# Weight sums for the modulation: computed and moved by GpSimd instead of VectorE and SyncE

## The chip, the cores and the metric

One NeuronCore of one Trainium2 chip runs the whole program. The metric is the device time of one execution, in microseconds (us). Before the change the median of 3 runs is 3883.19 us (3877.04 to 3884.56). Engines are named as in the profile: PE (TensorE matmul), PEld (its weight load), DVE (VectorE), ACT (ScalarE), POOL (GpSimd), SP (SyncE, which here only issues DMAs).

## The reference

A token sequence of 256 x 1024 goes through `first_block` (two layers: a gated feed-forward, an RWKV-7 and attention mixer, a second feed-forward) and then through `second_block` (two layers with a modulation of the norms and residuals, and a mixture over 16384 experts). What the change touches is small:

```python
# second_block, per layer l; c and c_ctx have 1024 elements, mod_w[l] is 1024 x 6144
m  = jax.nn.silu(c)     @ mod_w[l] + mod_b[l]     # 6 rows of 1024
mc = jax.nn.silu(c_ctx) @ mod_w[l] + mod_b[l]     # only layer 0, only its first 2048 columns
```

`m` does not depend on `x`, so the kernel makes most of it during `first_block`.

## The kernel before, in words

Activations lie with 128 tokens on the partitions. A large product streams its weights: `stream` (L581) takes one weight tile after another through two raw buffers (`raw_weights`, slots u = 0 and 1). For each tile SP issues the load, ACT rounds it to a high part (L634), DVE subtracts to get the low part (L658, both tiles of SBUF are read), and PE multiplies high and low parts (L449 to L451, three matmuls for each product). SP may load tile t+2 into a slot once DVE has made the low part of tile t. ACT may write the high part of tile t+2 once PE is done with tile t.

A feed-forward (`swiglu`, L816) is two such streams with 11 tiles each. The first (`linear_turned_stage`, ffn_in, 2 MB a tile, two DMAs) also has, for each tile, two sigmoid-gates on ACT and six DVE operations that finish `hidden` and its two parts. The second (`linear_sum_stage`, ffn_out, 1 MB a tile) accumulates in PSUM and adds to the residual at its end. `first_layer` (L1594) calls `swiglu` twice, and is run for l = 0 and 1 by a hardware loop. So there are eight feed-forward streams; here they are called A (first ffn_in), B (first ffn_out), C (second ffn_in) and D (second ffn_out), in each of the two layers.

`SideSums` (L529) works beside these four streams. The modulation weights of layer l are cut into 24 tiles of 128 x (8 x 256), 1 MB each. Partition p of block k holds row 128k + p. For each tile the eight blocks are multiplied by the partition's own condition value (`k.cond`, column k) and summed to 128 x 256; the sum over the partitions follows much later (`modulations`, L1655). The first 8 tiles are also summed with a second set of conditions (for `ctx`). Before the change the tiles are split 6, 6, 6, 6 over A, B, C and D, so A has 6 tiles with two sums, B has 2 with two sums and 4 with one, C and D have 6 with one.

The order is written out by hand. DVE makes a side tile after the low part and the finish of a weight tile: a `tensor_scalar` and seven `scalar_tensor_tensor` for each sum, 128 x 256 each. SP, after the load of weight tile t, waits in `SideSums.step` for side tile t-2 to be summed, loads the side tile two further on, and stores the sums to HBM:

```python
for t in range(2, tiles):
    load(t, t % 2, t // 2)      # waits for DVE's low part, issues the weight tile
    side.step(sp, t - 2)        # waits for DVE's side sum, issues load and stores
```

All its semaphores are in the set that POOL clears at the end of each stage (`k.clear`). A stage is a block at whose end all engines meet. POOL has no work in any of these stages. Later, in `experts` (L2117), it issues the 512 indirect DMAs that gather expert rows.

Of the kernel before, what the change touches and what calls it, by code (L numbers as in the profile page):

```python
# [11 lines left out]
ALU = mybir.AluOpType  # L12
# [3 lines left out]
P = 128  # L16
D = 1024
SEQ = 256
NT = SEQ // P
KC = D // P  # L20
# [12 lines left out]
NF = D_FF // P  # L33
# [90 lines left out]
class Ops:  # L124
# [3 lines left out]
    def __init__(self, nc, eng, vector):  # L128
        self.nc, self.eng, self.on_vector = nc, eng, vector
# [74 lines left out]
class Kernel:  # L204


    def __init__(self, nc, ctx, sems):
        self.nc, self.ctx = nc, ctx
        self.sem, self.names = Semaphores(nc, ctx, sems), 0

        self.rows = [ctx.enter_context(nc.semaphore(f"row{r}")) for r in range(RING)]
        self.row_uses = [0] * RING


        self.arrived = [ctx.enter_context(nc.semaphore(f"arrived{u}")) for u in range(2)]
        self.fills = [0, 0]
        self.preloaded = False
# [311 lines left out]
class SideSums:  # L529

    COLS = 256

    def __init__(self, k, tiles, sums, ctx_sums, which, both, room):
        self.k, self.tiles, self.sums, self.ctx_sums, self.which, self.both = k, tiles, sums, ctx_sums, which, both
        self.w, self.acc = room

    def load(self, sp, i):  # L540
        if i < len(self.which):
            sp.dma_start(self.w[:, i % 2, :], self.tiles[self.which[i]]).then_inc(self.k.sem[f"side_in{i % 2}"], 16)

    def stores(self, i):
        return 16 * sum(1 + (n < self.both) for n in self.which[:i])

    def step(self, sp, i):
        if i >= len(self.which):
            return
        sp.wait_ge(self.k.sem["side_done"], i + 1)  # L550
        self.load(sp, i + 2)
        n = self.which[i]
        cs = slice(n * self.COLS, (n + 1) * self.COLS)
        sp.dma_start(self.sums[:, cs], self.acc[:, i % 2, 0]).then_inc(self.k.sem["side_out"], 16)
        if n < self.both:
            sp.dma_start(self.ctx_sums[:, cs], self.acc[:, i % 2, 1]).then_inc(self.k.sem["side_out"], 16)

    def end(self, sp):
        sp.wait_ge(self.k.sem["side_out"], self.stores(len(self.which)))

    def make(self, o, i):
        if i >= len(self.which):
            return
        k, n, C = self.k, self.which[i], self.COLS
        o.eng.wait_ge(k.sem[f"side_in{i % 2}"], 16 * (i // 2 + 1))
        if i >= 2:

            o.eng.wait_ge(k.sem["side_out"], self.stores(i - 1))
        for kc_ in range(KC):
            o.eng.drain()  # L570
            w = self.w[:, i % 2, kc_ * C:(kc_ + 1) * C]
            for who in range(2 if n < self.both else 1):
                acc, c = self.acc[:, i % 2, who], k.cond[:, who * KC + kc_:who * KC + kc_ + 1]
                if kc_ == 0:
                    last = o.ts(acc, w, c, ALU.mult, free=True)
                else:
                    last = o.stt(acc, w, c, acc, ALU.mult, ALU.add, free=True)
        last.then_inc(k.sem["side_done"], 1)


def stream(k, block, wts, ahead, size, parts, done, done_per, finish_steps, act_steps=None, side=None):  # L581
# [5 lines left out]
    nc = k.nc  # L587
# [12 lines left out]
    @block.sync  # L600
    def _(sp):
        for t in range(first, min(2, tiles)):
            wts.load(k, sp, t, t)

        def load(t, u, m):

            sp.wait_ge(low, t + (PIECES - 2))
            wts.load(k, sp, t, u)

        if side is None:  # L610
            steps(sp, 2, tiles, load)
        else:
            side.load(sp, 0)
            side.load(sp, 1)
# [7 lines left out]
        if side is not None:  # L622
            side.end(sp)


    @block.scalar
    def _(act):
# [22 lines left out]
    @block.vector  # L650
    def _(dve):
        o = Ops(nc, dve, True)

        def part(t, u, m):
            for n, cs in enumerate(pieces(t)):

                dve.wait_ge(high, n + 1 if isinstance(t, int) and t == 0 else t + PIECES)
                nc.vector.tensor_tensor(parts.lo[:, u, cs], k.raw[:, u, cs], parts.hi[:, u, cs].bitcast(F32),  # L658
                                        ALU.subtract).then_inc(low, 1)

        part(0, 0, 0)

        def both(t, u, m):
            part(t, u, m)
            finish_steps(dve, o, t - 1, 1 - u)

        if side is None:
            steps(dve, 1, tiles, both)
        else:
# [146 lines left out]
def swiglu(k, gain, w_in, w_out, ahead, side_part):  # L816

    with ExitStack() as c:
        size = KC * SideSums.COLS
        room = k.sb("side_weights", [P, 2, size], ctx=c), k.sb("side_sums", [P, 2, 2, SideSums.COLS], ctx=c)  # L820
# [772 lines left out]

def first_layer(k, l, a, lam_tab):  # L1594
    def side(*which):
        return lambda part, room: SideSums(k, a["mod_tiles"][l], a["mod_sums"][l], a["ctx_mod_sums"][l], which[part], 8, room)

    row = lambda name: a[name][bass.ds(l, 1), :]
    mat = lambda name: a[name][l]
# [517 lines left out]
def experts(k, a, h, choice, mod, qT, skT, ring):  # L2117
# [9 lines left out]
    with ExitStack() as c:  # L2127
# [111 lines left out]
        for g in range(total):  # L2239
# [9 lines left out]

SEMAPHORES = (["loaded", "turned", "copied_v", "copied_s", "squared", "rooted", "reduced", "summed", "drained",  # L2250
               "used", "pre_done", "biased", "squashed", "exped", "masked", "lsum", "prod", "got", "corr",
               "grown", "done", "stored", "dotted", "gates_ready", "written", "chosen", "gate_exped", "side_in0", "side_in1",
               "side_done", "side_out", "part_in0", "part_in1", "part_in2"]
              + ["high", "low"] + [f"{e}_lane{g}" for e in ("pe", "act", "dve") for g in range(2)])


# [62 lines left out]
```

## Time and profile before

| | |
|---|---|
| median of 3 runs | 3883.19 us |
| profiled execution, whole | 3885.68 us |
| its span of instructions | 3883.8 us |
| granted TensorE clock, mean | 0.882 of full |
| PE, DVE, ACT, POOL busy | 2923.0, 2435.3, 1220.8, 590.0 us |
| DVE busy with side sums | 207.3 + 21.2 us |
| streams A to D, first layer | 23 to 181, 181 to 268, 808 to 954, 954 to 1037 us |
| streams A to D, second layer | 1052 to 1209, 1209 to 1297, 1839 to 1985, 1985 to 2068 us |

Times in rows are microseconds from the start of the span unless marked ns. A busy share is an average over stages with different limits. "[x <-E op Lnnn]" behind a row of a timeline is how long the engine was idle before it and which instruction let it go on. "issue" and "PEq" releases are sequencer time or the meeting at a stage's end. The granted clock has two levels, 0.5 (1.2 GHz) and 1 (2.4 GHz), and a stretch shows their mean.

### The profile page before, as it was taken

To read this page: it belongs to the slowest core of one execution; us is meant where nothing else is said; L and a number is where in the kernel's file an instruction comes from. 1 tells how busy PE (TensorE), PEld (TensorE's weight loads), DVE (VectorE), ACT (ScalarE), POOL (GpSimd) and SP (SyncE) were. 2 spreads that over 40 slices of the span, in tenths; PEclk is the share of its full clock that TensorE was granted. 3 is DMA by queue.
4 is the path that set the end of the run, shared out by engine and by line. 5 is a ranking of instruction groups with operands and counts; after the bars stand their busy time and mean duration, and the time that the engine had idled before them with its cause. 6 is when DMAs were issued, how large, how long until landed. Compare 5 with 4: busy or idle time off the path is not lost. (4 is left out here: it accounts for less than half of the span.)

```text
span 3883.8 us, 51747 instructions
## 1 busy us (share of the span) xinstructions
PE 2923.0 (75%) x18657; PEld 2090.2 (54%) x18657; DVE 2435.3 (63%) x4676; ACT 1220.8 (31%) x2422; POOL 590.0 (15%) x516
## 2 busy tenths in 40 slices
PE   6879684689788886936986688677777676777776
PEld 6859484478687785825973557322232272232222
DVE  6655665566586457555764445777777457777774
ACT  3223201333322321023321222344444324444443
POOL 0000000000000000000000000444444204444442
PEclk9989896689899897957997758899999988999999
DMA  6555100155665540003655303899999839999997
GB/s 224 181 197 182 38 3 33 60 200 194 213 199 192 166 146 2 3 32 130 221 190 212 106 6 115 355 421 421 421 421 421 330 106 376 421 421 421 421 419 306
DMA packets 266369, 866.70 MB, mean 223 GB/s; under 512 B 15128, under 2 KB 170912, under 8 KB 193440
## 3 DMA queue, kind: packets, MB, share of 16 engines
q0 software_dynamic: 73728, 536.90, 33.3%
q1 hardware_dynamic: 192416, 326.98, 24.6%
q8 instruction: 119, 1.95, 0.2%
q14 instruction: 106, 0.87, 0.1%
HBM read 854.39 MB, written 9.44 MB: 222 GB/s over the span
## 5 line engine op out<-in xcount | busy, mean ns | idle before, releaser
L658 DVE TENSOR_TENSOR weight_parts_lo<-raw_weights,weight_parts_hi 128x512 fp32r<-128x512 f32 (+7 forms) x224 | 497.0, 2242 | 302.7 <-ACT weight_parts_hi L634 302.7
L2147 POOL DMA_INDIRECT raw_weights<-peer_rows,expert_ids x208 | 239.9, 1153 | 2849.6 <-DVE expert_ids L151 2579.9
L634 ACT CAST weight_parts_hi<-raw_weights 128x512 fp32r<-128x512 f32 (+7 forms) x224 | 409.5, 1862 | 671.9 <-PE banks L451 258.4
L449 PE MATMUL banks<-normedT_hi,weight_parts_hi 128*128 128x256 f32 x1664 | 488.5, 294 | 68.5 <-DVE weight_parts_lo L658 68.5
L2235 PE MATMUL banks<-raw_weights,diagonals 128*128 128x512 f32 x832 | 401.9, 621 | 149.9 <-ACT diagonals L184 149.5
L2235 PE MATMUL banks<-expert_rows,diagonals 128*128 128x512 f32 x816 | 401.5, 630 | 119.3 <-ACT diagonals L184 118.3
L450 PE MATMUL banks<-normedT_lo,weight_parts_hi 128*128 128x256 f32 x1664 | 484.5, 291 | 0.0
L451 PE MATMUL banks<-normedT_hi,weight_parts_lo 128*128 128x256 f32 x1664 | 483.8, 291 | 0.0
L449 PEld LDWEIGHTS banks<-normedT_hi,weight_parts_hi 128*128 128x128 f32 x1664 | 334.0, 201 | 75.0 <-DVE weight_parts_lo L658 75.0
L2235 PEld LDWEIGHTS banks<-raw_weights,diagonals 128*128 128x128 f32 x832 | 151.8, 194 | 396.2 <-ACT diagonals L184 225.9
L2235 PEld LDWEIGHTS banks<-expert_rows,diagonals 128*128 128x128 f32 x816 | 150.5, 197 | 367.8 <-ACT diagonals L184 235.9
L160 DVE CUSTOM_DVE_ANT_0 products<-raw_weights,normed 128x1024 f32<-128x1024 f32 x208 | 254.9, 1226 | 140.9 <-DMA raw_weights<-peer_rows,expert_ids 130.2
L160 DVE CUSTOM_DVE_ANT_0 products<-expert_rows,normed 128x1024 f32<-128x1024 f32 x204 | 250.1, 1226 | 137.2 <-DMA expert_rows<-peer_rows,expert_ids 126.2
L450 PEld LDWEIGHTS banks<-normedT_lo,weight_parts_hi 128*128 128x128 f32 x1664 | 333.9, 201 | 0.0
L451 PEld LDWEIGHTS banks<-normedT_hi,weight_parts_lo 128*128 128x128 f32 x1664 | 333.5, 200 | 0.0
L184 ACT ACTIVATE gelu<-dots 128x1 f32<-128x1 f32 x512 | 103.5, 202 | 669.6 <-DVE dots L160 669.1
L2147 POOL DMA_INDIRECT expert_rows<-peer_rows,expert_ids x204 | 238.7, 1170 | 274.6 <-PE banks L2235 263.0
L2235 PE MATMUL banks<-queries,diagonals 128*128 128x512 f32 x400 | 199.1, 634 | 58.4 <-ACT diagonals L184 57.9
L156 DVE SCALAR_TENSOR_TENSOR side_sums<-side_weights,conditions,side_sums 128x256 f32<-128x256 f32 x448 | 207.3, 483 | 25.9 <-issue 0.9
L184 ACT ACTIVATE diagonals<-constants,coefficients 128x128 f32<-128x128 f32 x512 | 205.6, 402 | 36.8 <-issue 1.5
L449 PE MATMUL banks<-weight_parts_hi,hiddenT_hi 128*128 128x512 f32 x352 | 154.2, 438 | 64.7 <-DVE weight_parts_lo L658 64.7
L449 PE MATMUL banks<-weight_parts_hi,normedT_hi 128*128 128x344 f32 (+1 forms) x576 | 190.4, 331 | 10.4 <-DVE weight_parts_lo L658 10.4
(390 smaller groups left out, 4951.1 us busy)
## 6 DMA issues: line engine op xcount, KB each, us to landing
raw_weights<-ffn_in SPq DMA_DIRECT2D x88, 1024.0 KB, 8.0
side_weights<-mod_tiles SPq DMA_DIRECT2D x48, 1024.0 KB, 5.3
raw_weights<-ffn_out SPq DMA_DIRECT2D x44, 1024.0 KB, 7.0
raw_weights<-w_in SPq DMA_DIRECT2D x32, 1376.0 KB, 6.1
raw_weights<-peer_w_q SPq DMA_DIRECT2D x16, 1024.0 KB, 5.4
raw_weights<-w_branch SPq DMA_DIRECT2D x8, 1024.0 KB, 7.0
raw_weights<-w_out SPq DMA_DIRECT2D x8, 1024.0 KB, 5.0
raw_weights<-attn_in_w SPq DMA_DIRECT2D x4, 1792.0 KB, 7.3
```

Of the source, the lines that this page charges most:

```text
L156: return self.nc.vector.scalar_tensor_tensor(out=out, in0=a, scalar=s, in1=b, op0=op0, op1=op1)
L160: return self.nc.vector.tensor_tensor_reduce(out=out, in0=a, in1=b, scale=1.0, scalar=0.0, op0=ALU.mult, op1=ALU.add, accum_out=total)
L184: return self.nc.scalar.activation(out, a, func, bias=bias, scale=scale, **kw)
L449: nc.tensor.matmul(out, lhs.hi, rhs.hi, start=start, stop=False)
L450: nc.tensor.matmul(out, lhs.hi, rhs.lo, start=False, stop=False)
L451: return nc.tensor.matmul(out, lhs.lo, rhs.hi, start=False, stop=stop)
L634: nc.scalar.copy(parts.hi[:, u, cs], k.raw[:, u, cs]).then_inc(high, 1)
L658: nc.vector.tensor_tensor(parts.lo[:, u, cs], k.raw[:, u, cs], parts.hi[:, u, cs].bitcast(F32), ALU.subtract).then_inc(low, 1)
L2147: nc.gpsimd.indirect_dma_start(out=ring[r], out_offset=None, in_=table, in_offset=bass.IndirectOffsetOnAxis(ap=ids[:, n, t:t + 1], axis=0) ...
L2235: last = nc.tensor.matmul(k.bank(2 * j + half), diag[:, g % DIAGS, :], ring[g % RING][:, D + half * BANK:D + (half + 1) * BANK], start=t = ...
```

## The change

The side sums leave DVE and SP. A POOL program runs beside the other engines in each of the four streams. It fetches a side tile with its own DMA, one tile ahead, multiplies the whole 128 x 2048 tile in one operation by the eight conditions, each spread over 256 columns, and adds the halves three times (1024, 512 and 256 columns). For tiles with two sums the same is done in a second buffer. The stores are POOL's too, and before it goes on to the next tile it waits until they have landed. The tiles are split 5, 3, 10 and 6 over A, B, C and D, so that A and B have only tiles with two sums and C and D only tiles with one. The semaphores are new ones outside the cleared set, and waited for with counts that grow with l. SP and DVE in these streams run the plain loop (`steps`), as in streams without side work.

```diff
+    def fetch(self, pool, i):
         if i < len(self.which):
-            sp.dma_start(self.w[:, i % 2, :], self.tiles[self.which[i]]).then_inc(self.k.sem[f"side_in{i % 2}"], 16)
...
+            n = self.which[i]
+            pool.dma_start(self.w[:, i % 2, :], self.tiles[n]).then_inc(self.k.side_in[n % 2], 16)
+    def wait_stored(self, pool, n):
+        pool.wait_ge(self.k.side_out, self.l * (16 * (self.TILES + self.BOTH)) + 16 * (n + min(n, self.BOTH)))
...
-        for kc_ in range(KC):
-            o.eng.drain()
-            w = self.w[:, i % 2, kc_ * C:(kc_ + 1) * C]
-            for who in range(2 if n < self.both else 1):
-                acc, c = self.acc[:, i % 2, who], k.cond[:, who * KC + kc_:who * KC + kc_ + 1]
-                if kc_ == 0:
-                    last = o.ts(acc, w, c, ALU.mult, free=True)
-                else:
-                    last = o.stt(acc, w, c, acc, ALU.mult, ALU.add, free=True)
-        last.then_inc(k.sem["side_done"], 1)
+    def make(self, pool):
+        k, C, nc = self.k, self.COLS, self.k.nc
+        self.fetch(pool, 0)
+        for i, n in enumerate(self.which):
+            if i > 0:
+                self.wait_stored(pool, n)
+            self.fetch(pool, i + 1)
+            self.wait_fetched(pool, n)
+            w = self.w[:, i % 2, :]
+            parts = lambda ap: ap.rearrange("p (k n) -> p k n", k=KC)
+            if n < self.BOTH:
+                nc.gpsimd.tensor_tensor(parts(self.other), parts(w), spread(k.cond[:, KC:2 * KC], C), ALU.mult)
+                pool.drain()
+            nc.gpsimd.tensor_tensor(parts(w), parts(w), spread(k.cond[:, 0:KC], C), ALU.mult)
+            for width in (4 * C, 2 * C, C):
+                pool.drain()
+                for to in ([self.other, w] if n < self.BOTH else [w]):
+                    nc.gpsimd.tensor_tensor(to[:, 0:width], to[:, 0:width], to[:, width:2 * width], ALU.add)
+            pool.drain()
+            cs = slice(n * C, (n + 1) * C)
+            pool.dma_start(self.sums[:, cs], w[:, 0:C]).then_inc(k.side_out, 16)
+            if n < self.BOTH:
+                pool.dma_start(self.ctx_sums[:, cs], self.other[:, 0:C]).then_inc(k.side_out, 16)
+        self.wait_stored(pool, self.which[-1] + 1)
...
-            for t in range(2, tiles):
-                load(t, t % 2, t // 2)
-                side.step(sp, t - 2)
+        steps(sp, 2, tiles, load)
...
+    if side is not None:
+        @block.gpsimd
+        def _(pool):
+            side.make(pool)
...
-            for t in range(1, tiles):
-                both(t, t % 2, t // 2)
-                side.make(o, t - 1)
+        steps(dve, 1, tiles, both)
...
-           side(range(0, 6), range(6, 12)))
+           side(range(0, 5), range(5, 8)))
...
-    swiglu(k, row("norm_ffn2"), w_up, sum_weights(mat("ffn2_out"), NF), None, side(range(12, 18), range(18, 24)))
+    swiglu(k, row("norm_ffn2"), w_up, sum_weights(mat("ffn2_out"), NF), None, side(range(8, 18), range(18, 24)))
```

## Rows read from the trace of the kernel before

**Rows 1.** Timeline of ACT in stream A: start, length, instruction, [idle before <-releaser]

```profile
40.01 0.38 ACT L184 ACTIVATE silu_gate<-banks 128x256 f32<-128x256 f32 x1 [5.38 <-PE banks L451]
...
63.25 3.61 ACT L634 CAST weight_parts_hi<-raw_weights 128x4096 fp32r<-128x4096 f32 x1 [11.35 <-DMA raw_weights<-ffn_in]
...
178.84 0.38 ACT L184 ACTIVATE silu_gate<-banks 128x256 f32<-128x256 f32 x1 [5.37 <-PE banks L451]
```

**Rows 2.** Timeline of DVE in stream A

```profile
66.89 4.42 DVE L658 TENSOR_TENSOR weight_parts_lo<-raw_weights,weight_parts_hi 128x4096 fp32r<-128x4096 f32 x1 [3.59 <-ACT weight_parts_hi L634]
...
74.50 6.61 DVE L156 SCALAR_TENSOR_TENSOR side_sums<-side_weights,conditions,side_sums 128x256 f32<-128x256 f32 x14
```

**Rows 3.** Timeline of SP's DMA issues in stream A

```profile
81.67 0.35 SPq L542 DMA_DIRECT2D side_weights<-mod_tiles  x1
82.21 0.37 SPq L554 DMA_DIRECT2D mod_sums<-side_sums  x1
...
83.30 1.53 SPq L496 DMA_DIRECT2D raw_weights<-ffn_in  x2
```

**Rows 4.** Waits of SP's queue: us in total, times, longest us

```profile
SPq L542 <- DVE side_sums L156: 321.2, 32, 19.1
```

**Rows 5.** Windows: length, busy (x instructions) by engine, granted clock, DMA share, GB/s

```profile
25.00:31.00 6.00, 5.46 (x25) 5.46 (x26) 3.90 (x4) 4.46 (x4) 0.00 (x0) 0.50 1.07 396
...
23.00:181.00 158.00, 136.93 (x1056) 135.31 (x1056) 112.85 (x176) 48.85 (x38) 0.00 (x0) 0.92 0.58 193
181.00:268.00 87.00, 68.94 (x264) 53.73 (x264) 56.50 (x82) 20.96 (x14) 0.00 (x0) 0.90 0.60 217
808.00:954.00 146.00, 132.75 (x1056) 131.74 (x1056) 95.00 (x129) 48.72 (x37) 0.00 (x0) 0.95 0.58 193
954.00:1037.00 83.00, 70.59 (x264) 55.54 (x264) 50.67 (x66) 21.11 (x14) 0.00 (x0) 0.88 0.55 199
```

**Rows 6.** Timeline of ACT in a 4-tile sum stream without side work

```profile
767.42 3.98 ACT L634 CAST weight_parts_hi<-raw_weights 128x512 fp32r<-128x512 f32 x5 [1.34 <-PEq L458]
776.23 1.91 ACT L634 CAST weight_parts_hi<-raw_weights 128x2048 fp32r<-128x2048 f32 x1 [4.83 <-PE banks L451]
781.67 1.91 ACT L634 CAST weight_parts_hi<-raw_weights 128x2048 fp32r<-128x2048 f32 x1 [3.53 <-PE banks L451]
793.50 1.06 ACT L184 ACTIVATE junk<-residual 128x1024 f32<-128x1024 f32 x1 [9.93 <-PEq L736]
```

**Rows 7.** Groups by shape on DVE: busy us, mean ns | idle before, releasers

```profile
L658 DVE TENSOR_TENSOR weight_parts_lo<-raw_weights,weight_parts_hi 128x2048 fp32r<-128x2048 f32 x67 | 153.6, 2292 | 138.1 <-ACT weight_parts_hi L634 138.1
...
L137 DVE TENSOR_TENSOR normed<-normed,modulation 128x1024 f32<-128x1024 f32 x8 | 9.8, 1225 | 0.6
...
L658 DVE TENSOR_TENSOR weight_parts_lo<-raw_weights,weight_parts_hi 128x512 fp32r<-128x512 f32 x56 | 35.0, 687 | 13.1 <-ACT weight_parts_hi L634 13.1
...
L137 DVE TENSOR_TENSOR hiddenT_lo<-hidden,hiddenT_hi 128x256 fp32r<-128x256 f32 x88 | 37.4, 426 | 6.5
...
L174 DVE CAST hiddenT_hi<-hidden 128x256 fp32r<-128x256 f32 x88 | 26.0, 295 | 6.4
...
L160 DVE CUSTOM_DVE_ANT_0 products<-raw_weights,normed 128x1024 f32<-128x1024 f32 x208 | 254.9, 1226 | 140.9 <-DMA raw_weights<-peer_rows,expert_ids 130.2 <-issue 0.5
```

**Rows 8.** Groups of instructions on POOL, same columns

```profile
L2147 POOL DMA_INDIRECT raw_weights<-peer_rows,expert_ids x208 | 239.9, 1153 | 2849.6 <-DVE expert_ids L151 2579.9 <-PE banks L2235 263.6 <-issue 6.1
...
L2302 POOL MEMSET const-float32-1.0<- 128x1 f32 x1 | 0.1, 104 | 0.0
```

**Rows 9.** Timeline of DVE, a one-column fill

```profile
9.59 0.06 DVE L2269 MEMSET lambda_table<- 128x1 f32 x1
```

**Rows 10.** DMA issues by line: KB each, median us from issue to landing

```profile
side_weights<-mod_tiles SPq DMA_DIRECT2D x48, 1024.0 KB, 5.3
...
raw_weights<-ffn_out SPq DMA_DIRECT2D x44, 1024.0 KB, 7.0
```

**Rows 11.** The answer for tile side_sums, its stores' time to landing

```profile
DMA to landing us min/median/max: 1.7/5.0/6.2
```

More of the change, by code:

```diff
@@ L216, in __init__ @@
         self.fills = [0, 0]
+        self.side_in = [ctx.enter_context(nc.semaphore(f"side_in{u}")) for u in range(2)]
+        self.side_out = ctx.enter_context(nc.semaphore("side_out"))
         self.preloaded = False
@@ L534 @@
     COLS = 256
[L536 to L540, printed above, removed]
-        if i < len(self.which):
-            sp.dma_start(self.w[:, i % 2, :], self.tiles[self.which[i]]).then_inc(self.k.sem[f"side_in{i % 2}"], 16)
-    def stores(self, i):
-        return 16 * sum(1 + (n < self.both) for n in self.which[:i])
@@ L547, in step @@
[L547 to L568, printed above, removed]
-        for kc_ in range(KC):
-            o.eng.drain()
-            w = self.w[:, i % 2, kc_ * C:(kc_ + 1) * C]
-            for who in range(2 if n < self.both else 1):
-                acc, c = self.acc[:, i % 2, who], k.cond[:, who * KC + kc_:who * KC + kc_ + 1]
-                if kc_ == 0:
-                    last = o.ts(acc, w, c, ALU.mult, free=True)
-                else:
-                    last = o.stt(acc, w, c, acc, ALU.mult, ALU.add, free=True)
-        last.then_inc(k.sem["side_done"], 1)
+    BOTH = 8
@@ new lines, with __init__, wait_fetched @@
+    TILES = 6 * D // COLS
+    def __init__(self, k, l, tiles, sums, ctx_sums, which, room):
+        self.k, self.l, self.tiles, self.sums, self.ctx_sums, self.which = k, l, tiles, sums, ctx_sums, which
+        self.w, self.other = room
+    def fetch(self, pool, i):
+        if i < len(self.which):
+            n = self.which[i]
+            pool.dma_start(self.w[:, i % 2, :], self.tiles[n]).then_inc(self.k.side_in[n % 2], 16)
+    def wait_fetched(self, pool, n):
+        pool.wait_ge(self.k.side_in[n % 2], self.l * (8 * self.TILES) + 16 * (n // 2 + 1))
@@ L608, in load @@
             wts.load(k, sp, t, u)
[L610 to L614, printed above, removed]
-            for t in range(2, tiles):
-                load(t, t % 2, t // 2)
-                side.step(sp, t - 2)
+        steps(sp, 2, tiles, load)
         if ahead is not None:
@@ L621, in _ @@
                 ahead.load(k, sp, t, t)
-        if side is not None:
-            side.end(sp)
+    if side is not None:
+        @block.gpsimd
+        def _(pool):
+            side.make(pool)
     @block.scalar
@@ L665, in both @@
             finish_steps(dve, o, t - 1, 1 - u)
-        if side is None:
-            steps(dve, 1, tiles, both)
-        else:
-            for t in range(1, tiles):
-                both(t, t % 2, t // 2)
-                side.make(o, t - 1)
+        steps(dve, 1, tiles, both)
         finish_steps(dve, o, tiles - 1, (tiles - 1) % 2)
@@ L819, in swiglu @@
         size = KC * SideSums.COLS
-        room = k.sb("side_weights", [P, 2, size], ctx=c), k.sb("side_sums", [P, 2, 2, SideSums.COLS], ctx=c)
+        room = k.sb("side_weights", [P, 2, size], ctx=c), k.sb("side_products", [P, size], ctx=c)
         hT = split_sb(k, "normedT", [P, KC, SEQ], c)
@@ L1595, in side @@
     def side(*which):
-        return lambda part, room: SideSums(k, a["mod_tiles"][l], a["mod_sums"][l], a["ctx_mod_sums"][l], which[part], 8, room)
+        return lambda part, room: SideSums(k, l, a["mod_tiles"][l], a["mod_sums"][l], a["ctx_mod_sums"][l], which[part], room)
     row = lambda name: a[name][bass.ds(l, 1), :]
@@ L2251 @@
                "used", "pre_done", "biased", "squashed", "exped", "masked", "lsum", "prod", "got", "corr",
-               "grown", "done", "stored", "dotted", "gates_ready", "written", "chosen", "gate_exped", "side_in0", "side_in1",
-               "side_done", "side_out", "part_in0", "part_in1", "part_in2"]
+               "grown", "done", "stored", "dotted", "gates_ready", "written", "chosen", "gate_exped", "part_in0", "part_in1", "part_in2"]
               + ["high", "low"] + [f"{e}_lane{g}" for e in ("pe", "act", "dve") for g in range(2)])
```

## The prediction

> **What bounds the kernel now.** I read the timeline of ACT in stream A first, because ACT is the first engine that touches a weight tile and its idle time names what is late. The gates come 5.76 us apart (5.38 idle + 0.38 busy) where PE is the only limit, which is 11.5 us for a tile [rows 1]. In the middle of the stream that pace is lost: ACT idles 11.35 us for a weight tile to land [rows 1]. The timelines of DVE and SP say why the tile was late. DVE had finished the low part at 71.3 us, so the slot was free [rows 2], but SP issued that slot's next load only at 83.3 us, behind the side tile and the two stores for which it had waited until DVE finished the sums at about 81.1 us [rows 2, 3]. SP's waits show how general this is: 321.2 us in 32 waits for side sums alone [rows 4]. So what costs time is not DVE's 228 us of side work as such, but that weight loads stand behind it in SP's order.
>
> How much is lost, stream by stream: in A the second gate is at 40.01 and the last, the 22nd, at 178.84. At PE's pace the last would be at 40.01 + 20 x 5.76 = 155.2, so 23.6 us are lost and A would take 158 - 23.6 = 134.4 [rows 1, 5]. C has the same matmuls and takes 146: 11.6 lost [rows 5]. A sum stream of four tiles without side work takes 793.5 - 767.4 = 26.1 us with rounds 5.44 apart, each waiting for PE [rows 6]. With 11 tiles that is 26.1 + 7 x 5.44 = 64.2, against 87 in B and 83 in D: 22.8 and 18.8 lost [rows 5]. One layer: 474 now, 397.2 at PE's pace. The second layer's streams are within 1 us of these, so the most that can be gained is 2 x 76.8 = 154 us.
>
> **The change, part by part.** (1) *Leaves DVE and SP.* Weight loads follow the low part at once. In A a slot is needed again after two tiles, 23 us. From low part to low part it needs about 0.5 issue, 8 to 9 for 2 MB (the 5.3 of one 1 MB tile, and more behind it), 3.6 rounding and 4.4 low part, 17 to 18 [rows 1, 2, 10]. In B it is 0.5 + 5.3 + 1.9 + 2.3 = 10 of 10.9, and 11.7 with the 7.0 us that a 1 MB load takes now beside a side tile [rows 6, 7, 10]: there the cover is thin, some 1 us for each tile that POOL's fetch collides with. The loops on SP and DVE cost nothing in A and C, where DVE has 6.9 of 11.5 us filled. The 154 us are thus freed if POOL keeps up.
>
> (2) *Added on POOL.* Everything meets at the stage's end, so a stream lasts as long as the longer of PE's work and POOL's chain; nothing else is queued behind POOL's waits but the clearing of semaphores. The trace shows no elementwise work on POOL. The nearest rows: DVE needs 2.29, 1.23, 0.69 and 0.43 us for two-input operations of 2048, 1024, 512 and 256 columns, 4.63 for the product and three additions of one sum [rows 7]. The only operation that both engines do is a one-column fill, 104 ns on POOL and 60 on DVE [rows 8, 9]. Lower bound: DVE's own 4.63. Upper bound: three times that, 13.9. I take 1.8 times, by the fills: 8.3 us for one sum, 16.7 for two.
>
> The Trainium skill, GPSIMD Engine Reference, section "Elementwise — side-by-side cycle accounting", states 4497 against 2293 ns for a 2048-column addition, 1.96 times; no row here shows it. By it one sum would be 9.1 us, and the whole about 48 us longer where POOL is the bound.
>
> Around the arithmetic each tile has one or two store issues and a fetch issue at 1.15 us (the indirect DMA's time on POOL, the only POOL DMA in the trace) [rows 8]. Then comes the wait until the stores have landed, which nothing covers because the next fetch and product stand behind it. SP's stores landed in 1.7 to 6.2 us, median 5.0, right behind a 1 MB load in the same queue [rows 11]; without that load ahead I take 3. With 0.4 to 0.5 for drains, a tile with one sum takes 1.15 + 3 + 1.15 + 8.3 + 0.4 = 14.0 us, one with two sums 2.3 + 3 + 1.15 + 16.7 + 0.5 = 23.7. The first tile of a stream waits for its own fetch too, 1.15 + 5.3 = 6.5 [rows 8, 10]. POOL's chains: A 6.5 + 5 x 23.7 = 125, B 6.5 + 3 x 23.7 = 77.6, C 6.5 + 10 x 14 = 146.5, D 6.5 + 6 x 14 = 90.5. So already without any disturbance POOL hides only in A.
>
> (3) *What the two engines do to each other.* In A and C DVE has, for each tile, a low part of 4.42 us reading two SBUF tiles, two subtractions of 0.43 that do the same, and two SBUF-to-SBUF casts of 0.295 [rows 2, 7], 5.9 us, 64.5 us in 11 tiles; in B and D 2.29 a tile, 25 us. POOL's operations also read two SBUF operands. If such operations take turns, POOL's chain grows by DVE's time for the share of it in which POOL computes: A 0.67 x 64.5 = 43, B 0.64 x 25 = 16, C 0.57 x 64.5 = 37, D 14. Bounds: nothing, and all of this. The rows that come nearest don't decide it: with two SBUF inputs DVE needs 1226 ns for 1024 columns while POOL issues indirect DMAs, and 1225 while it does not [rows 7], so making descriptors disturbs nobody; but that doesn't read tiles. I take two thirds, since the lower bound needs the second SBUF input of DVE to cost POOL nothing at all.
>
> That turn-taking is a rule of the Trainium skill: SBUF — State Buffer, section "Who interferes with whom", says that a DVE instruction with two SBUF inputs contends with a GpSimd instruction that reads SBUF, and that the loser waits for the whole instruction. By it the full bound holds, and no trace here shows both at work.
>
> Sum: A 125 + 29 = 154, B 77.6 + 11 = 88, C 146.5 + 25 = 171, D 90.5 + 9 = 100, together 513 against 474. [...] (513 - 474 + 6) x 2 = +90. The profiled execution took 3885.7 us (span 3883.8), 2.5 above the median of the runs, so 3976.
>
> **The rivals.** *No contention* (25%): the chains stand as in (2): 134.4, 77.6, 146.5, 90.5 = 449, with 3 for the clock after C: -22 a layer, 3885.7 - 44 = 3842. For it: DVE's unchanged 1226 ns. Against it: only reads would contend, and there are none there. *POOL hides everywhere* (14%): from about DVE's own speed (4.63 a sum: 10.3 a tile in C and D, 16 in A and B: 86, 55, 110, 68) the weight streams set the end except for a few us in D: 3732, to 3760 with fetches colliding in B and D. Against it: the fill's 104 against 60 ns. *POOL at three times DVE* (8%): 19.6 and 34.9 us a tile, 181, 111, 202 and 124 even without contention: +144 + 10 a layer, 4194. *The forecast* (53%): POOL's chain and its turns with DVE set the end of B, C and D. With full turns 168 + 94 + 183.5 + 104.5 = 550, +163, 4049. The point from which it turns to the other side is a disturbed tile of about 14 us in C and D and 28 in A and B; I expect 17 and 30.
>
> **How the numbers follow.** Predicted 3976. The forecast alone spans 3880 to 4060. For 8 in 10 the range goes down into POOL hiding everywhere and up past full turns: 3750 to 4090. About 0.2% (8 us) is what a measurement of this kernel can tell from no change. Slower: 0.50 of the forecast, 0.02 of no contention, 0.08 of the slow POOL, 0.60. Same: 0.02 + 0.02, 0.04. Faster: 0.01 of the forecast, 0.21 and 0.14 of the first two rivals, 0.36.
>
> **What would show it.** Right: ACT's waits for weight tiles in A all but gone and gates 5.76 us apart until about 160 us; then PE, DVE and ACT idle until POOL is done; POOL's 2048-column product at 4 to 5 us where DVE is idle and longer, or with a gap before it, where a low part runs; the low part's mean above 4.42. Wrong: POOL finishing before PE in C (contention absent, or POOL faster than 1.8 times), a product of under 3 us, or stores landing in 2 us. If gates are not at 5.76 us in A although SP is free, POOL's operations hold up DVE's low parts for more than the 4.6 us a tile that DVE has to spare, and step (1) is wrong.

## The result and the profile after

| | before | after |
|---|---|---|
| median of 4 runs | 3881.93 us | 3925.66 us (3917.37 to 3933.27) |
| ratio | 1 | 1.0114, 95% interval 1.0089 to 1.0139 |
| profiled execution, span | 3885.68, 3883.8 us | 3917.37, 3915.8 us |
| stream A, first layer | 157.7 us | 161.7 us |
| stream B | 87.5 | 83.3 |
| stream C | 145.7 | 147.3 |
| stream D | 86.8 | 101.8 |
| A to D | 477.7 | 494.1 |

A stream is measured here, in every kernel, from ACT's first rounding of it to ACT's first instruction behind it. The change made the kernel slower: by 32 us in the profiled pair, 44 in the medians. Two layers of 16.4 us more in the streams are 32.8 us, so the streams hold all of the profiled difference. The forecast was 90.

Windows of the kernel after (the columns of [rows 5]): the last busy figure is now POOL's, which was zero.

```profile
23.00:185.00 162.00, 131.98 (x1056) 130.76 (x1056) 116.18 (x81) 49.18 (x37) 115.15 (x55) 0.92 0.53 181
185.00:268.00 83.00, 62.33 (x264) 50.25 (x264) 34.83 (x18) 21.14 (x14) 64.84 (x33) 0.89 0.55 196
809.00:957.00 148.00, 135.72 (x1056) 134.12 (x1056) 134.25 (x81) 48.98 (x37) 98.98 (x60) 0.94 0.65 222
957.00:1060.00 103.00, 64.34 (x264) 51.10 (x264) 40.15 (x18) 22.29 (x16) 61.74 (x36) 0.84 0.45 166
```

Read DVE's column (the third) in the C window. It has lost its side sums, 129 instructions have become 81, and yet its busy time rose from 95.0 to 134.3 us of 148. The groups by shape on DVE say where that comes from; the low parts and the finish of `hidden` are the same instructions as in [rows 2, 7], only longer:

```profile
L658 DVE TENSOR_TENSOR weight_parts_lo<-raw_weights,weight_parts_hi 128x4096 fp32r<-128x4096 f32 x40 | 208.2, 5205 | 24.0 <-ACT weight_parts_hi L634 23.6
L658 DVE TENSOR_TENSOR weight_parts_lo<-raw_weights,weight_parts_hi 128x2048 fp32r<-128x2048 f32 x67 | 192.1, 2868 | 156.7 <-ACT weight_parts_hi L634 156.7
L174 DVE CAST hiddenT_hi<-hidden 128x256 f32 x80 | 142.7, 1784 | 13.3 <-issue 13.3
L137 DVE TENSOR_TENSOR hiddenT_lo<-hidden,hiddenT_hi 128x256 f32 x80 | 86.3, 1079 | 11.8 <-issue 0.6
...
L137 DVE TENSOR_TENSOR hidden<-silu_gate,banks 128x256 f32<-128x256 f32 x88 | 36.1, 411 | 31.7 <-ACT silu_gate L184 31.7
```

4423 ns became 5205, 2292 became 2868, and the small ones grew most: the cast from 295 ns to 1784, the subtraction from 426 to 1079 (80 of the 88 each; the profile lists the other 8 apart). The product with the gate, which reads only one operand from SBUF and the other from PSUM (`banks`), has not grown: 411 ns, 416 before. A busy DVE is here a DVE that waits inside its instruction.

The timeline of POOL in A, with the second side tile:

```profile
64.28 0.54 POOL L549 DMA_DIRECT2D side_weights<-mod_tiles  x1 [5.98 <-DMA ctx_mod_sums<-side_products]
64.84 3.62 POOL L571 TENSOR_TENSOR side_products<-side_weights,conditions 128x2048 f32<-128x2048 f32 x1
72.79 3.60 POOL L573 TENSOR_TENSOR side_weights<-side_weights,conditions 128x2048 f32<-128x2048 f32 x1 [4.33 <-issue]
76.53 6.41 POOL L577 TENSOR_TENSOR side_products<-side_products 128x1024 f32<-128x1024 f32 x1
...
88.95 4.91 POOL L577 TENSOR_TENSOR side_weights<-side_weights 128x256 f32<-128x256 f32 x1
...
102.47 0.54 POOL L549 DMA_DIRECT2D side_weights<-mod_tiles  x1 [6.77 <-DMA ctx_mod_sums<-side_products]
```

From fetch to fetch 38.2 us. Three things stretch it: the wait for the stores (5.98 and 6.77), 4.33 us between two products that depend on nothing outside POOL, and additions that take 6.41 and 4.91 us where undisturbed ones take 2.34 and 0.72. ACT's timeline shows what that chain costs at the end of A and D:

```profile
39.21 0.39 ACT L184 ACTIVATE silu_gate<-banks 128x256 f32<-128x256 f32 x1 [5.06 <-PE banks L453]
...
158.37 0.38 ACT L184 ACTIVATE silu_gate<-banks 128x256 f32<-128x256 f32 x1 [5.38 <-PE banks L453]
164.12 0.38 ACT L184 ACTIVATE silu_gate<-banks 128x256 f32<-128x256 f32 x1 [5.37 <-PE banks L453]
185.25 3.99 ACT L634 CAST weight_parts_hi<-raw_weights 128x512 fp32r<-128x512 f32 x5 [20.74 <-PEq L770]
...
1058.83 1.06 ACT L184 ACTIVATE junk<-residual 128x1024 f32<-128x1024 f32 x1 [42.85 <-issue]
```

The gates of A are done at 164.5, earlier than before (179.2 [rows 1]), and 20.7 us pass until POOL has finished. At PE's pace the last gate would start at 39.21 + 20 x 5.76 = 154.4; it starts at 164.12, so A's weight stream loses 9.7 us even with SP free. D waits 42.85 us, its own last round included.

### The profile page after: what moved, and what is told of

It is laid out like the page before. It is cut to its first block and busy times, and to the rows that moved or that the text cites. A ratio compares the mean times of both kernels' runs of the same rounds, so it can differ in the third digit from the quotient of the medians.

```text
span 3915.8 us, 51915 instructions
## 1 busy us (share of the span) xinstructions
PE 2892.7 (74%) x18657; PEld 2068.1 (53%) x18657; DVE 2452.9 (63%) x4164; ACT 1221.9 (31%) x2422; POOL 1281.3 (33%) x884
## 5 line engine op out<-in xcount | busy, mean ns | idle before, releaser
L658 DVE TENSOR_TENSOR weight_parts_lo<-raw_weights,weight_parts_hi 128x512 fp32r<-128x512 f32 (+7 forms) x224 | 566.8, 2554 | 297.6 <-ACT weight_parts_hi L634 297.2
L549 POOL DMA_DIRECT2D side_weights<-mod_tiles x48 | 25.9, 539 | 1255.8 <-issue 1150.2
L577 POOL TENSOR_TENSOR side_weights<-side_weights 128x1024 f32<-128x1024 f32 x144 | 254.6, 1768 | 41.7 <-issue 33.1
L573 POOL TENSOR_TENSOR side_weights<-side_weights,conditions 128x2048 f32<-128x2048 f32 x48 | 196.8, 4101 | 50.9 <-issue 28.6
```

What stands on the lines that cost most here:

```text
L549: pool.dma_start(self.w[:, i % 2, :], self.tiles[n]).then_inc(self.k.side_in[n % 2], 16)
L573: nc.gpsimd.tensor_tensor(parts(w), parts(w), spread(k.cond[:, 0:KC], C), ALU.mult)
L577: nc.gpsimd.tensor_tensor(to[:, 0:width], to[:, 0:width], to[:, width:2 * width], ALU.add)
```

## The experiments

Two theories stood against each other. **S** (from step 1): what costs time before the change is SP's order, the weight load behind the side tile's step, and not DVE's work. **V**: DVE's side work itself holds up the low parts. For the time after the change, **T**: instructions of POOL and DVE take turns, one waiting for the whole of the other; **P**: POOL's own waits (stores, fetches) make its chain long. **R** sharpens T: only reads take turns. **D** explains the gap: POOL's drain waits for DMAs that POOL itself has queued.

**1. DVE keeps the sums, POOL moves the tiles.** Split 6, 6, 6, 6 as before.

```diff
-            side.make(pool)          # after: fetch, sum and store on POOL
+            side.move(pool)          # fetch and store on POOL, waits for side_done
...
+            for t in range(1, tiles):
+                both(t, t % 2, t // 2)
+                side.make(o, t - 1)  # the sums of before, on DVE
```

> The kernel before (split 6, 6, 6, 6, sums on DVE), but POOL issues the side tiles' fetches and stores; SP has only the weight loads. Theory S (what the old kernel lost, it lost because weight loads stood behind side waits in SP's order): DVE then limits only where its own work exceeds PE's tile time. A: 4.4 + 2.3 + 7.3 = 14.0 against 11.5 us in 6 tiles, 149 us; B 77; C 10.9 against 11.5, so PE's pace, 134; D 71. Together 431 against 474 a layer, -86 us, ratio to the kernel before 0.978. Rival V (DVE's 228 us of side work are what costs): the same work on the same engine, ratio 1.00 within 0.3%.

Measured: 3805.12 us, ratio 0.9803 (0.9784 to 0.9822); A 150.6, B 75.5, C 134.0, D 75.7. S holds for the larger part: with DVE's side work unchanged and only the queue changed, 76 us are gained, and C runs at PE's pace. A does not (150.6 against 134): the expectation named the reason, DVE's own 14.0 us beside a tile of two sums, and experiment 9 returns to it.

**2. The kernel before, with SP's side step behind the next weight load.**

```diff
             for t in range(2, tiles):
                 load(t, t % 2, t // 2)
-                side.step(sp, t - 2)
+                if t > 2:
+                    side.step(sp, t - 3)
+            side.step(sp, tiles - 3)
...
+        if i > 0:                    # in step(), ahead of a tile's stores
+            sp.wait_ge(self.k.sem["side_out"], self.stores(i))
```

> The kernel before with one edit of order: SP handles side tile t-3 instead of t-2 behind the load of weight tile t, so that the wait for DVE's sum has long been met when SP gets there. Nothing moves to another engine. Theory S: nearly all of what e1 gives, ratio 0.978 to 0.982. Rival V: 1.00. A third possibility, that POOL's own DMA queue matters (the weight loads stand behind 1 MB side tiles in SP's queue): e2 keeps that, so e2 would be 0.99 where e1 is 0.978.

Measured: 3795.20 us, 0.9775 (0.9758 to 0.9792); A 148.6, B 74.9, C 133.9, D 74.3. It needs no other engine at all, and the third possibility of the expectation, that POOL's own queue matters (0.99), is out. SP's issues in A show how the order of [rows 3] has changed: the side tile and its stores now go out before the weight slot is free, and the weight load follows at once when it is.

```profile
62.90 0.35 SPq L542 DMA_DIRECT2D side_weights<-mod_tiles  x1
63.43 0.37 SPq L556 DMA_DIRECT2D mod_sums<-side_sums  x1
64.00 0.35 SPq L558 DMA_DIRECT2D ctx_mod_sums<-side_sums  x1
67.64 1.03 SPq L496 DMA_DIRECT2D raw_weights<-ffn_in  x2
```

**3. The kernel after without POOL's arithmetic.** One 256-column product a sum is left of it; the sums are not made.

```diff
-                nc.gpsimd.tensor_tensor(parts(self.other), parts(w), spread(k.cond[:, KC:2 * KC], C), ALU.mult)
+                nc.gpsimd.tensor_tensor(self.other[:, 0:C], w[:, 0:C], w[:, 0:C], ALU.mult)
...
-            for width in (4 * C, 2 * C, C):   # and the tree of sums
```

> The changed kernel, but of POOL's arithmetic only a product of 256 columns a sum is left (the rest of the modulation sums is left out, so the output is not the reference's); fetches, stores and all waits stay. Both theories of the changed kernel (POOL's chain as the bound, or DVE waiting its turn) expect the streams at PE's pace: 397 a layer, 3732 us, ratio 0.961. POOL's chain of DMA waits alone, some 9 us a tile, is 100 of 134 us in C. If it is above 0.975, part (1) of the prediction was too large: something other than SP's order holds the weight streams.

Measured: 3739.36 us, 0.9631 (0.9613 to 0.9648); A 133.1, B 66.8, C 133.9, D 69.9. So the change gives 142 us back by clearing SP and DVE, and POOL's arithmetic costs 186 (3925.66 - 3739.36).

**4. The store wait hidden.** In tiles with one sum the last addition goes to the second buffer, and the wait for the stores stands ahead of it instead of ahead of the next fetch.

```diff
-            if i > 0:
+            if i > 0 and n < self.BOTH:
                 self.wait_stored(pool, n)
...
+                if n >= self.BOTH and width == C:
+                    if i > 0:
+                        self.wait_stored(pool, n)
+                    nc.gpsimd.tensor_tensor(self.other[:, 0:C], w[:, 0:C], w[:, C:2 * C], ALU.add)
+                    continue
```

> The changed kernel, but for tiles with one sum (all of C and D) the last addition goes to the second buffer, so that the next fetch and product don't wait for the store; that wait stands ahead of the next tile's last addition. A and B unchanged. Theory P (POOL's undisturbed chain is the bound of C and D, DVE's low part fits in POOL's own pauses): 2.7 us a tile less in C until the weight stream's 134 us is met, and 3 to 4 in D: C 136, D 80 against 147 and 101, ratio to the kernel before 0.995. Theory T (the turns with DVE are the bound of C): the pause in which DVE's low part ran is gone, the two must share: C stays at 145 to 150, D about 90, ratio 1.005.

Measured: 3916.69 us, 1.0094 (1.0075 to 1.0112), within the error of the kernel after; A 161.2, B 82.3, C 153.4, D 92.0. D gained 10 us and C lost 6 (12 in the second layer), which neither theory had: P said 136 for C, T 145 to 150. Two lines of POOL's timeline in C tell why it is no clean verdict: the fetch follows the store without a wait now, but the next addition stands off by 4.94 us.

```profile
861.01 3.62 POOL L572 TENSOR_TENSOR side_weights<-side_weights,conditions 128x2048 f32<-128x2048 f32 x1
869.57 3.90 POOL L581 TENSOR_TENSOR side_weights<-side_weights 128x1024 f32<-128x1024 f32 x2 [4.94 <-issue]
```

The wait went, and another took its place, behind the product. That gap is D's subject: the fetch issued at 860.46 took 8.9 us to land, at 869.36, and the addition starts at 869.57.

**5. POOL writes only.** Products and additions become fills of the same places, two for each, about as long; the output is then not the reference's.

```diff
-                    nc.gpsimd.tensor_tensor(to[:, 0:width], to[:, 0:width], to[:, width:2 * width], ALU.add)
+                    for _ in range(2):
+                        nc.gpsimd.memset(to[:, 0:width], 0.0)
+                        pool.drain()
```

> The changed kernel, but POOL's arithmetic is replaced by fills (two for each product and each addition, same shapes; a 16-column product is left in front), so POOL writes SBUF for a similar time but hardly reads it (the modulation sums are left out). Theory R (the turns are taken for the second read): DVE's low parts and subtractions are back at 4.42 and 0.43 us, and only the SBUF-to-SBUF casts, which run at more than one column a cycle, may still wait. The weight streams in A and C are at PE's pace. Rival W (any work of POOL on SBUF blocks DVE): the low part's mean stays near 5.2 us. Time: if the fills take less than the products, 3740 to 3790, ratio 0.963 to 0.977, in either case less telling than the means.

Measured: 3986.95 us, 1.0282 (1.0264 to 1.0299); A 151.1, B 80.8, C 185.6, D 111.0. The time missed every expectation, the mechanism didn't. DVE's groups:

```profile
L666 DVE TENSOR_TENSOR weight_parts_lo<-raw_weights,weight_parts_hi 128x4096 fp32r<-128x4096 f32 x40 | 177.0, 4425 | 74.0 <-ACT weight_parts_hi L642 74.0
...
L174 DVE CAST hiddenT_hi<-hidden 128x256 f32 x80 | 45.3, 566 | 13.5 <-issue 13.5
```

The low part is back at 4425 ns beside an engine that fills for about 8 us a tile, and the two do meet: one that starts at 864.84 and takes 4.42 us has POOL's fill of 868.18 beside it. A two-input instruction of DVE waits for POOL's reads, not for its writes. That is R for these instructions, and it is what the Trainium skill, SBUF — State Buffer, section "Who interferes with whom", states. R does not hold for the cast: it still takes 566 ns on the mean against 295, and one of 0.91 us starts at 873.30, while POOL fills, so it does wait for writes. The same section says that casts, in the two-port mode that they can enter, contend with GpSimd. Where the time went is on POOL:

```profile
859.21 0.54 POOL L549 DMA_DIRECT2D side_weights<-mod_tiles  x1 [2.12 <-DMA mod_sums<-side_weights]
859.76 0.23 POOL L576 TENSOR_TENSOR side_weights<-side_weights 128x16 f32<-128x16 f32 x1
868.18 1.81 POOL L579 MEMSET side_weights<- 128x2048 f32 x1 [8.19 <-issue]
```

The product of 2048 columns had covered most of the fetch's flight. With 16 columns in its place POOL stands idle for 8.19 us in the drain behind it, and that fetch took 8.8 us to land: 859.21 + 8.8 = 868.0. The kernel after shows the same in A. Of the fetch issued at 64.28 the trace says:

```profile
DMA to landing us min/median/max: 8.2/8.2/8.2
```

64.28 + 8.2 = 72.48, and the next product starts at 72.79. Three more fetches of that kernel (the last in B) agree: issued at 102.47 with 9.0, next instruction at 111.70; 138.50 with 5.1, 143.84; 218.33 with 6.6, 225.23.

**6. Experiment 1 with the work spread.** The tiles split 5, 3, 10, 6 and placed in every second weight tile in A, in every one in C.

```diff
+    def slots(self):
+        return {10: list(range(1, 11)), 5: [1, 3, 5, 7, 9], 6: [1, 2, 4, 5, 7, 8], 3: [1, 4, 7]}[len(self.which)]
...
-                side.make(o, t - 1)
+                if t in side.slots():
+                    side.make(o, side.slots().index(t))
```

> As e1 (DVE sums, POOL issues the DMAs), but with the split 5, 3, 10, 6 and the two-sum tiles made beside every second weight tile in A and every third in B, two of three in D. DVE then needs 20.8 of 23.0 us for two tiles in A, 14.2 of 16.3 for three in B, 10.9 of 11.5 in C, 15.3 of 16.3 in D. Theory S: everything within PE's pace but for some queueing, 3745 us, ratio 0.965 (0.962 to 0.972). Rival V: no better than e1's 0.980.

Measured: 3813.29 us, 0.9828 (0.9811 to 0.9844); A 151.4, B 78.9, C 133.8, D 75.7. A miss. Fewer tiles in A and B did not shorten them.

**7. Experiment 2 with the work spread in the same way** (the `slots` of experiment 6, in SP's step and in DVE's).

> As e2 (DVE sums, SP issues everything, its side step only where DVE's sum is already done), with the same split and spacing as e6. Theory S: as e6, ratio 0.965 (0.962 to 0.972); the small gain of e2 over e1 (0.9775 against 0.9803) may show again. Rival V: no better than e2's 0.9775.

Measured: 3803.03 us, the median of three runs (a fourth took 8733 us and is left out), 0.9801 (0.9781 to 0.9820); A 150.9, B 77.2, C 133.9, D 72.3. The same miss. In DVE's timeline in A the reason can be read:

```profile
69.08 6.61 DVE L156 SCALAR_TENSOR_TENSOR side_sums<-side_weights,conditions,side_sums 128x256 f32<-128x256 f32 x14
75.61 4.42 DVE L667 TENSOR_TENSOR weight_parts_lo<-raw_weights,weight_parts_hi 128x4096 fp32r<-128x4096 f32 x1
```

A tile with two sums is one piece of 7.3 us (68.39 to 75.6) that starts only when the finish of the weight tile is done. The low part is ready for DVE at 70.65 (ACT's rounding, 67.03 + 3.62) and waits for the piece. Two weight tiles last 23 us, and DVE's own work in them with the sums is 2 x 6.9 + 7.3 = 21: the sums are not too long, the block is. C has ten blocks of 4.2 us and loses nothing.

**8. The kernel after with small fetches.** From the third tile of a stream on only 8 columns are fetched; those sums are then not the reference's.

```diff
+            if i < 2:
                 pool.dma_start(self.w[:, i % 2, :], self.tiles[n]).then_inc(self.k.side_in[n % 2], 16)
+            else:
+                pool.dma_start(self.w[:, i % 2, 0:8], self.tiles[n][:, 0:8]).then_inc(self.k.side_in[n % 2], 16)
```

> The changed kernel, but from the third side tile of a stream on the fetch brings only 8 columns (so later tiles sum stale weights). Theory D (a drain on POOL also waits until the DMAs that POOL has queued are done, so the drain behind the first product waits for the next tile's 1 MB): the gap behind the first product, 4 to 5 us in A and 1.1 in C, becomes 0.3 to 0.5; A gets about 12 us shorter, B 2.5, C at most 6, D 8; with both layers 45 to 55 us less than the changed kernel, ratio to the kernel before about 0.998. Rival L (the gap comes from the turns with DVE): it stays, and the ratio is 1.006 to 1.011.

Measured: 3903.09 us, 1.0062 (1.0045 to 1.0079); A 152.4, B 82.4, C 143.4, D 99.3. POOL's timeline in C:

```profile
864.52 3.75 POOL L576 TENSOR_TENSOR side_weights<-side_weights,conditions 128x2048 f32<-128x2048 f32 x1
868.59 4.99 POOL L580 TENSOR_TENSOR side_weights<-side_weights 128x1024 f32<-128x1024 f32 x3 [0.32 <-issue]
```

The fetch lands in 1.8 us, within the product, and the gap is 0.32 us instead of 1.1: D holds. In A the fetches of 8 columns issued at 64.88 and 120.21 still took 5.4 and 5.8 us to land, and the next product began 0.3 us behind each landing, which says the same. In time the edit is worth 23 us where 45 to 55 were expected: C's tile only went from 13.6 to 13.05 us (3.9 us in all), D gained 2.5 of the expected 8, and A fell by 9.3 us in the first layer but not in the second (161.6, and 161.0 in the kernel after).

**9. Experiment 7 with one sum a weight tile.** The two sums of a tile are made in two weight tiles; 10, 6, 10, 6 sums in A, B, C, D.

```diff
+    def units(self):
+        return [(i, who) for i, n in enumerate(self.which) for who in range(2 if n < self.both else 1)]
...
-                    side.make(o, side.slots().index(t))
+                    side.make_unit(o, side.slots().index(t))   # one (i, who)
```

> The sums stay on VectorE and SyncE issues everything, as in the kernel before, but SyncE's side step stands behind the weight load of two tiles later, and one sum (never two) is made a weight tile: 10, 6, 10 and 6 of them in streams A, B, C and D of a layer. If VectorE's piece of two sums (7.3 us at a stretch) is what kept A and B over TensorE's 134 and 66 us in the version that only spread the tiles (150.9, 77.2, 133.9, 72.3), then A comes to 134 to 137, B to 67 to 70, C stays at 134, D at 70 to 72: ratio to before 0.965 to 0.970. Rival: something else in A holds the lower halves back (the weights' own arrival beside the side tile's megabyte): A stays over 145, ratio 0.978 or more.

Measured: 3749.59 us, 0.9664 (0.9651 to 0.9677), 5 runs of 3747.41 to 3751.38. Windows of the four streams, first layer:

```profile
23.38:156.77 133.39, 129.00 (x1056) 128.79 (x1056) 109.73 (x160) 49.17 (x38) 0.00 (x0) 1.00 0.66 218
156.77:226.12 69.35, 64.11 (x264) 50.84 (x264) 50.30 (x66) 21.13 (x14) 0.00 (x0) 0.95 0.63 226
766.20:900.14 133.94, 129.55 (x1056) 129.35 (x1056) 109.73 (x160) 48.97 (x38) 0.00 (x0) 0.97 0.74 245
900.14:973.00 72.86, 64.15 (x264) 51.13 (x264) 50.40 (x66) 21.13 (x14) 0.00 (x0) 0.95 0.62 228
```

A falls from 150.9 to 133.4. DVE is busy for 110 of 133 us and PE for 129: the sums fit beside the weight work, in pieces of 4.2 us. The number of sums in each stream is that of experiment 7, so the gain over it is that of the smaller pieces. This is only 10 us above experiment 3, in which nobody makes the sums. It beats both kernels, by 130 us and 176 us.

**10. The kernel after with both of POOL's waits shortened,** the edits of 4 and 8 together (again not the reference's sums).

> The changed kernel with both of GpSimd's waits shortened: in C and D the store is waited for one product later, and from the third tile of a stream on only 8 columns of the side tile are fetched (those sums are then not the reference's). GpSimd's own chain of a one-sum tile is then its 7.9 us of arithmetic with about 1.5 us of issue. If its two-input instructions and VectorE's take full turns, a tile of C needs at least 7.9 us and VectorE's 5.2 to 5.9 us one after the other, 13.1 to 13.8 us: C stays at 141 to 148 although GpSimd waits for nothing. If the slow C came from GpSimd's waits, the tile falls to TensorE's 11.5 us and C to 134. A, whose two-sum tiles change only in their fetch: 150 to 153. Ratio 1.003 to 1.010 by the first, 0.992 by the second.

Measured: 3890.96 us, 1.0030 (1.0017 to 1.0044); A 160.5, B 82.3, C 152.7, D 87.6. T's ratio came, and C stayed far above 134. Rows of POOL, then of DVE, in C:

```profile
842.99 0.53 POOL L552 DMA_DIRECT2D side_weights<-mod_tiles  x1
843.54 6.71 POOL L575 TENSOR_TENSOR side_weights<-side_weights,conditions 128x2048 f32<-128x2048 f32 x1
850.58 4.11 POOL L584 TENSOR_TENSOR side_weights<-side_weights 128x1024 f32<-128x1024 f32 x2 [0.32 <-issue]
854.89 5.01 POOL L581 TENSOR_TENSOR side_products<-side_weights 128x256 f32<-128x256 f32 x1 [0.20 <-issue]
```

```profile
842.37 4.42 DVE L665 TENSOR_TENSOR weight_parts_lo<-raw_weights,weight_parts_hi 128x4096 fp32r<-128x4096 f32 x1
...
847.29 3.12 DVE L174 CAST hiddenT_hi<-hidden 128x256 f32 x1 [0.17 <-issue]
...
854.89 4.41 DVE L665 TENSOR_TENSOR weight_parts_lo<-raw_weights,weight_parts_hi 128x4096 fp32r<-128x4096 f32 x1
```

Turns of whole instructions: POOL's product stands until the low part ends (842.37 + 4.42 = 846.8) and then runs its 3.6 us, during which DVE's cast of 0.3 us stands to 850.4. A 256-column addition that meets a low part at 854.89 takes 5.01 us instead of 0.74. In the middle of C POOL now waits for stores or fetches 2.6 us a tile at most and still needs 14 to 18 us a tile; in the kernel after, with its waits, it was 13.6. Where the waits are shortened the turns take their place. I had C at 141 to 148 and got 152.7, and A at 150 to 153 and got 160.5, although POOL's program in A is the same as in experiment 8: which engine meets which there is decided by microseconds, and shifts 8 us. The two layers show it inside one run: A took 160.5 and 152.1 us here, 152.4 and 161.6 in experiment 8.

## Why the direction was right and the size wrong

**Step (1), what is freed, holds in its size, and in its cause for the larger part.** 154 us were named as what SP's order costs, with PE's pace at 134.4 and 64.2. Experiment 3 has 133.1 and 133.9 in A and C, 66.8 and 69.9 in B and D, and 142 us in all; of the rest the thin cover is at least a part (in B of experiment 3 ACT still waits four times for a weight load, 2.1 to 7.1 us). SP's waits for side sums [rows 4] are gone after the change. But experiments 1 and 2, which mend only the order, gave 76 and 86 us of it. Of the other 56 at least 46 were DVE's side work after all: in A of experiment 2 its low parts start at 62.66, 76.79 and 90.92, 14.13 us apart with no idle time between them, and making one sum a tile (experiment 9) gave 46 us over experiment 2. "Not DVE's 228 us of side work as such" was too strong.

**Step (2), POOL's own chain: the arithmetic right, all around it off.** An undisturbed tile with two sums runs from 164.41 to 181.06, 16.65 us where 16.7 was taken; one with one sum from 1042.71 to 1051.13, 8.4 where 8.3 was. (The fill's ratio of 1.8 was luck in its parts: the product is 3.60 against 4.1, the addition of 1024 columns 2.34 against 2.2.) By the figure of the Trainium skill cited there, 4497 ns for an addition of 2048 columns, the product would be 0.9 us longer than the 3.60 measured; no addition of that width ran. A DMA issue costs POOL 0.54 to 0.60 us, not the 1.15 of an indirect one. The stores are waited for 2.09 us in C and 6 to 6.8 in the middle of A, not 3. Two steps were missed: 0.74 us ahead of each store, and the drain that waits for the fetch in flight, 1.1 in C and up to 5.06 in A.

**Step (3), the turns, failed for C, and this is the error in the forecast.** The mechanism was right, the place where it bites was not. I charged the turns to POOL's chain: 146.5 + 25 = 171, 2.5 us for each of ten tiles. C took 147.3, and in its middle POOL lost 0.3 us a tile (3.77 for 3.60 in the product, 4.73 for 4.60 in the additions), DVE 6.4. POOL's timeline in C, and DVE's beside it:

```profile
860.54 0.53 POOL L549 DMA_DIRECT2D side_weights<-mod_tiles  x1 [2.09 <-DMA mod_sums<-side_weights]
861.09 3.77 POOL L573 TENSOR_TENSOR side_weights<-side_weights,conditions 128x2048 f32<-128x2048 f32 x1
865.95 4.73 POOL L577 TENSOR_TENSOR side_weights<-side_weights 128x1024 f32<-128x1024 f32 x3 [1.09 <-issue]
871.42 0.60 POOL L580 DMA_DIRECT2D mod_sums<-side_weights  x1 [0.74 <-issue]
874.10 0.53 POOL L549 DMA_DIRECT2D side_weights<-mod_tiles  x1 [2.09 <-DMA mod_sums<-side_weights]
```

```profile
856.43 4.96 DVE L658 TENSOR_TENSOR weight_parts_lo<-raw_weights,weight_parts_hi 128x4096 fp32r<-128x4096 f32 x1
...
861.89 3.12 DVE L174 CAST hiddenT_hi<-hidden 128x256 f32 x1 [0.16 <-issue]
...
866.07 2.43 DVE L174 CAST hiddenT_hi<-hidden 128x256 f32 x1 [0.17 <-issue]
868.65 1.43 DVE L137 TENSOR_TENSOR hiddenT_lo<-hidden,hiddenT_hi 128x256 f32 x1
870.00 4.96 DVE L658 TENSOR_TENSOR weight_parts_lo<-raw_weights,weight_parts_hi 128x4096 fp32r<-128x4096 f32 x1
```

Both engines repeat after 13.57 us. POOL's product and additions take 8.5 us, hardly more than alone; DVE's long low part starts with POOL's last addition and falls for the rest into the 4 us in which POOL stores and waits. What waits is DVE: 0.5 us in the low part, 2.8 and 2.1 in the two casts, 1.0 in a subtraction. With its 6.9 us of work that makes 13.4 of the 13.57. So in C the two engines have locked, DVE has next to no idle time left (134 of 148 us busy), and weight tiles pass every 13.57 us instead of 11.5. Not POOL's tail but the weight stream itself sets the end (ACT is idle for 1.6 us before D's first rounding, against 20.7 before B's), and that is a way of losing time that the forecast did not have. POOL's tile, 14.0 + 2.5 in the forecast, takes the same 13.57. It is as full as DVE's, so the rows do not show which of the two sets the period; when experiment 8 took 0.8 us from POOL's gap, the period fell by 0.5.

**A: 161.7 against 154.** The second tile took 38.2 us where the forecast had 23.7 + 5.8 = 29.5: turns 8.3 instead of 5.8 (6.41 and 4.91 above for 2.34 and 0.72), the missed drain 4.0 over the 0.3 of an undisturbed tile, the stores 3.8 more, the gap before them 0.7, less 1.8 for the issues and 0.5 for the sums. The third took 36.0. The last two, with the weight stream at its end or over, took 25.9 and 21, so only 8 us are left of it. **B: 83.3 against 88, D: 101.8 against 100.** In both the terms change but nearly cancel: D's second to fourth tiles take 17.1, 19.5 and 14.3 us against 15.5, its last two 12.6 and about 10.

**The clock term was too large.** The sum has 6 us a layer for the clock behind two tails in which PE has nothing to do, and no run shows that term. The window of B's first 6 us, behind A's tail of 20.7 us (the last figures are granted clock, DMA share, GB/s):

```profile
185.25:191.25 6.00, 4.61 (x14) 3.58 (x15) 4.48 (x5) 3.98 (x5) 1.07 (x2) 0.62 0.63 224
```

In the same stretch before, 180.5 to 186.5, the clock was 0.72: 0.6 us are lost. At the starts of D and of the next layer's A there is no difference, 0.72 and 0.72, 0.50 and 0.50.

Together, for both layers, from the forecast's +90: C takes off 47.4, the clock 12 at most, B 9.4, and the sum before, 474 by windows and 477.7 by ACT's marks, 7.4; A and D put back 15.4 and 3.6. That leaves 33, and the profiled pair differs by 32.

**Of the rivals,** no contention (3842) is refuted by the groups on DVE and by experiment 5. "POOL hides everywhere" was wrong for POOL's speed, but its price is what the change would have been worth: 3739 in experiment 3. Of what the forecast named as signs, the idle tail in A and the low part above 4.42 came. The undisturbed product took 3.6 us, neither the 4 to 5 of the forecast nor under 3. "POOL finishing before PE in C" came too, listed as a sign of no contention. It was contention, on the other engine. Stores waited for 2.09 us in C were another of the signs against. And the last sign came in part: A's gates fell 9.7 us behind PE's pace although SP was free, so POOL did hold up DVE's low parts there too, hidden behind POOL's tail.

What stays open: why the lock of 13.57 us forms in C and not in A, which engine sets its period, and what makes the stores slow beside weight loads: in A, after the last load, the same two were waited for only 1.8 us. None of these was tried.

## What to carry to other kernels

Before moving work to an idle engine, ask what its old place cost: here the order of one queue, and one line of order on SP (experiment 2) gave 86 us while the work stayed where it was; cut into pieces that fit between two deadlines (experiment 9), it gave 130. Work on GpSimd that reads SBUF ran here not beside but in turn with VectorE's instructions that read two SBUF tiles and with its casts within SBUF, for whole instructions on both sides, so charge it to both, and look first at VectorE's shortest instructions, which can wait tenfold. When two engines take turns in a loop, ask which period they lock to, rather than adding the turns to one of them.

## What the runs showed of the hardware that I had not expected

- POOL's drain waits for the DMAs POOL has queued: eight fetches that landed 5.1 to 9.0 us after issue each let the next instruction go 0.2 to 0.3 us later, and a fetch that landed in 1.8 us left a gap of 0.32.
- A cast of 0.295 us on DVE waited for POOL's writes as well (0.566 mean beside fills), the two-input subtraction only for its reads (4425 against 5205 ns).
- A fill of 2048 columns takes POOL 1.81 us, a product of the same width with spread conditions 3.60.
- The two stores of a tile were waited for 6 to 6.8 us in the middle of A and 1.8 us at its end.
